# The causal mask of an attention kernel, added by TensorE into the scores' bank instead of by VectorE in its maximum

## The reference: three mixers in one layer, two of them attention

```python
def safe_softmax(s, mask):
    s = jnp.where(mask, s.astype(jnp.float32), NEG_INF)
    m = jnp.max(s, axis=-1, keepdims=True)
    e = jnp.where(mask, jnp.exp(s - m), 0.0)
    return e / jnp.maximum(jnp.sum(e, axis=-1, keepdims=True), 1e-30)
...
    s = (jnp.einsum('bqhd,bshd->bhqs', qb, k).astype(jnp.float32) * ATTN_SCALE
         + cb[..., None] - c[:, :, None, :])
    mask = s_pos[None, :] <= t[:, None]
    p = safe_softmax(s, mask)
    return jnp.einsum('bhqs,bshd->bqhd', p, v).astype(q.dtype)
```

## Time and profile before

| | |
|---|---|
| time, median of 3 runs | 481.15 us (481.06 to 481.26) |
| the profiled execution's own time | 481.06 us |
| its span | 479.3 us (1.8 us lie outside it) |
| busy | TensorE 448.9 us (94%), weight loads 337.2, VectorE 309.1 (64%), ScalarE 249.8, GpSimd 75.1 |
| mean granted TensorE clock | 0.972 of full |
| nsa's attention | about 162 to 237 us |
| fox's attention | about 336 to 377 us |

### The profile page before, as it was taken

One profiled execution on the slowest core, in us unless ns is written; L12 is line 12 of the kernel. 1 busy time (PEld: TensorE's weight loads), 2 busy tenths in 40 slices (PEclk: granted clock), 3 DMA queues, 4 the chain that ended last, 5 costly groups with the idle time before them and its releaser, 6 DMA issues.

```text
span 479.3 us, 6533 instructions
## 1 busy us (share of the span) xinstructions
PE 448.9 (94%) x2232; PEld 337.2 (70%) x2232; DVE 309.1 (64%) x655; ACT 249.8 (52%) x472; POOL 75.1 (16%) x122
## 2 busy tenths in 40 slices
PE   5899999999869889999999999999799996999997
PEld 1576778788758665656577897988666675788885
DVE  5976469887987977777428854758867367522204
ACT  5555685667464666666528865842566435312200
POOL 4011240000000155556300000000354200000000
PEclk9899999999979989999999999999799998899999
DMA  7722234331141200000011242642200011922004
GB/s 260 290 89 88 88 89 131 102 118 45 44 133 44 88 2 1 1 3 0 2 44 45 88 125 96 166 144 83 93 2 1 1 43 55 335 94 88 0 1 175
DMA packets 12960, 39.52 MB, mean 82 GB/s; under 512 B 1792, under 2 KB 2048, under 8 KB 12672
## 3 DMA queue, kind: packets, MB, share of 16 engines
q1 hardware_dynamic: 12928, 39.11, 25.1%
HBM read 32.81 MB, written 2.10 MB: 73 GB/s over the span
## 4 chain that ended last, share of the span: by engine, by line
PE 75%; DVE 14%; issue 4%; ACT 3%; POOL 1%; DMA 1%; SPq 1%; POOLq 0%; DVEq 0%; ACTq 0%
PE bank L1112 10%; PE bank L1114 10%; PE bank L1113 10%; PE bank L1225 6%; PE bank L1207 5%; PE bank L1325 5%; PE bank L1326 4%; PE bank L1327 4%; PE bank L1198 4%; PE bank L1199 3%; DVE wl L767 2%; PE bank L1123 2%; PE bank L1092 2%; PE bank L1142 2%; PE bank L1094 2%
## 5 line engine op out<-in xcount | busy, mean ns | idle before, releaser
L1112 PE MATMUL bank<-xh,wh 128*128 128x512 f32 (+1 forms) x264 | 111.9, 424 | 0.0
L1114 PE MATMUL bank<-xh,wl 128*128 128x512 f32 (+1 forms) x264 | 104.1, 394 | 0.0
L1113 PE MATMUL bank<-xl,wh 128*128 128x512 f32 (+1 forms) x264 | 103.6, 392 | 0.0
L767 DVE TENSOR_TENSOR wl<-raw,wh 128x1024 fp32r<-128x1024 f32 x51 | 62.0, 1219 | 34.5 <-ACT wh L502 34.1
L502 ACT ACTIVATE wh<-raw 128x1024 fp32r<-128x1024 f32 x51 | 53.1, 1049 | 35.3 <-PE bank L1327 35.1
L952 DVE CUSTOM_DVE_ANT_0 bank<-bank,mask_row 128x128 f32<-128x128 f32 (+3 forms) x96 | 47.1, 495 | 24.1 <-PE bank L1199 23.5
L1112 PEld LDWEIGHTS bank<-xh,wh 128*128 128x128 f32 (+1 forms) x264 | 49.7, 188 | 15.0 <-issue 5.0
L1113 PEld LDWEIGHTS bank<-xl,wh 128*128 128x128 f32 (+1 forms) x264 | 49.4, 187 | 14.4 <-issue 4.0
L1114 PEld LDWEIGHTS bank<-xh,wl 128*128 128x128 f32 (+1 forms) x264 | 49.3, 187 | 11.7
L470 POOL TENSOR_SCALAR probs<-probs,rcp,gates 128x128 f32<-128x128 f32 (+3 forms) x52 | 31.7, 617 | 125.8 <-DVE rcp L968 125.6
L610 ACT ACTIVATE probs<-bank,negmax 128x256 f32<-128x256 f32 (+3 forms) x77 | 40.5, 527 | 20.0 <-DVE negmax L952 19.2
(11 more groups left out here) (199 smaller groups left out, 766.5 us busy)
## 6 DMA issues: line engine op xcount, KB each, us to landing
raw<-in_w_in SPq DMA_DIRECT2D x39, 512.0 KB, 3.4
raw<-in_w_out SPq DMA_DIRECT2D x12, 512.0 KB, 3.3
x_raw<-in_xT SPq DMA_DIRECT2D x8, 256.0 KB, 6.2
x_res<-in_x_tok SPq DMA_DIRECT2D x1, 2048.0 KB, 8.2
out_y<-y_out SPq DMA_DIRECT2D x8, 256.0 KB, 2.1
cmp_w_sb<-in_cmp_w SPq DMA_DIRECT2D x1, 1024.0 KB, 10.3
kh_fox<-kh_fox SPq DMA_DIRECT2D x8, 128.0 KB, 2.3
kl_fox<-kl_fox SPq DMA_DIRECT2D x8, 128.0 KB, 2.4
```

Source lines behind the costliest of these rows:

```text
L767: dve.tensor_tensor(wl[:, c % HL, :], raw[:, c % RAW, :], wh[:, c % HL, :].bitcast(F32), ALU.subtract).then_inc(wl_ready, 1)
L1112: pe.matmul(dst, hi, xh[:, k, :], start=(k == 0), stop=False)
L1113: pe.matmul(dst, hi, xl[:, k, :], start=False, stop=False)
L1114: mm = pe.matmul(dst, lo, xh[:, k, :], start=False, stop=(k == KT - 1))
```

## The change

The mask moves from VectorE's fused operation to a third (for fox a fourth) matmul in the same accumulation, and VectorE's operation becomes a plain maximum.

- TensorE: after L1199 a matmul of the identity (`ident_r`) with the causal triangle (`mask_r`), both 128 x 128 in fp32r, is added to the last 128 of the unit's n columns; `s_ready` is now given by it. 96 more matmuls with their weight loads.
- VectorE: a TENSOR_REDUCE (maximum, negated) that reads the bank and writes one number a row takes the place of the fused operation and its accumulator read: 96 instructions for 192. The bank is not written.
- ScalarE: the exponential loses its scale of -1.
- Set-up: `mask_row` is gone; `ones` has 128 columns of its own, GpSimd clears 384 columns less, VectorE makes `ident_r` and `mask_r` right after the second chunk's split, and the copy of the triangle at L1003 is gone.

```diff
-        mask_row = sb("mask_row", [P, SEQ])
-        ones = mask_row[:, SEQ - P:]
+        ones = sb("ones", [P, P])
+        ident_r = sb("ident_r", [P, P], F32R)
+        mask_r = sb("mask_r", [P, P], F32R)
...
-            nc.gpsimd.memset(mask_row[:, 0:SEQ - P], 0.0)
...
-                act.activation(probs_of(u, 0, n), SCORE[u % S_RING][:, 0:n], ACT.Exp, scale=-1.0,
+                act.activation(probs_of(u, 0, n), SCORE[u % S_RING][:, 0:n], ACT.Exp,
...
-                        scores = SCORE[s % S_RING][:, 0:n]
-                        dve.tensor_tensor_reduce(scores, scores, mask_row[:, SEQ - n:], scale=-1.0, scalar=3.0e38,
-                                                 op0=ALU.add, op1=ALU.min,
-                                                 accum_out=negmax[:, s % M_RING:s % M_RING + 1])\
-                           .then_inc(max_ready, 1)
+                        dve.tensor_reduce(negmax[:, s % M_RING:s % M_RING + 1], SCORE[s % S_RING][:, 0:n], AX.X,
+                                          ALU.max, negate=True).then_inc(max_ready, 1)
...
             dve.wait_ge(const_loaded, 16)
+            dve.tensor_copy(ident_r[:, :], ident)
+            dve.tensor_copy(mask_r[:, :], cst[:, CAUSAL:CAUSAL + P])
...
-            dve.tensor_copy(mask_row[:, SEQ - P:], cst[:, CAUSAL:CAUSAL + P])
...
-                pe.matmul(dst[:, 0:n], q, kl[:, 0:n], start=False, stop=True).then_inc(s_ready, 1)
+                pe.matmul(dst[:, 0:n], q, kl[:, 0:n], start=False, stop=False)
+                pe.matmul(dst[:, t * P:n], ident_r[:, :], mask_r[:, :], start=False, stop=True).then_inc(s_ready, 1)
```

More of the change, by code:

```diff
@@ L448, in _ @@
         def _(pool):
-            nc.gpsimd.memset(ones, 1.0).then_inc(ones_ready, 1)
+            nc.gpsimd.memset(ones[:, :], 1.0).then_inc(ones_ready, 1)
             nc.gpsimd.memset(eps1[:, :], EPS)
@@ L1253, in _ @@
                     square = qr[:, i % 2, :]
-                pe.matmul(MEAN[:, :], ones, square, start=(k == 0),
+                pe.matmul(MEAN[:, :], ones[:, :], square, start=(k == 0),
                           stop=(k == KT - 1)).then_inc(x_sq_used, 1)
```

## The result

The changed kernel takes 482.23 us (480.94 to 483.91), the kernel before, on the same chip, 479.55 us (478.02 to 481.29). The ratio is 1.0053, with a 95% interval of 1.0039 to 1.0068: 2.6 us slower, where 5.9 were forecast. The sign was right and the size was more than twice too large. Of the 4.8 us between the forecast's 487.0 and 482.23, 1.6 lie in its base: 481.15 was the median of three runs of the kernel before, and twenty give 479.55.

What follows compares the result with a forecast made beforehand. TensorE was taken to bound the settled pairs, VectorE having some 2 us slack. Masks 8.58, waits -1.7, VectorE -0.4 gave 6.5, shaded to 5.9; 481.1 + 5.9 = 487.0 us, range 483.0 to 490.5.

Steps and rivals of the forecast that it cites:

- One mask matmul: TensorE, each unit's added mask: 0.11 us at full clock whatever n is, 0.22 at half clock; 8.58 us for 71.
- lower bound: Mask matmul on TensorE: 0.06 us if only 128 columns stream and the weight load hides behind the matmul ahead.
- Nothing moves: Rival: a mask costs 0.06 us on TensorE and all waits return, giving about 482 us; chance 0.06.
- signs of being wrong: Pairs keeping their length, mask piece of 0.06 or 0.22, a stage's beginning without a 0.50-clock stretch, or a new one.
- back-to-back issue gap: Skill figure for TensorE: some 81 ns per sustained 128-column load and matmul; would make 71 masks about 2.4 us less.
- what TensorE gets back: Settled nsa pairs: transposes' waits for GpSimd shrink by 0.31 us a pair over 5.5 pairs, -1.7 us.
- fox's own 0.16: Fox pairs' transpose waits, 0.16 us over 2.1 pairs, counted only in the bound of -2.9 us.
- The shade of 0.6: Sum lowered by 0.6 us, from 6.5 to 5.9, towards the full return of TensorE's waits.
- VectorE, -0.4: Stage beginnings and ends: 0.05 us less latency for each of about eight maxima on the chain, -0.4 us.
- the clock stays up: Rival: masks keep TensorE at 2.4 GHz at stage beginnings, nsa 1.6 us, fox 3.1; middle 484 us, chance 0.11.
- the set-up: Before attention: VectorE's first work shifts by up to 0.4 us, covered by 1.4 us of projections; cost 0.

Runs made afterwards that it cites:

- the pads: Changed kernel with an unused tile of 4 or 64 bytes a partition ahead of the identity, moving later tiles: 484.34 us (1.0098) and 484.08 us (1.0089).
- VectorE's half alone: Changed kernel without the mask matmul: plain maximum, causal mask inside the diagonal block left out; 479.82 us, 0.9997 of the kernel before.
- the first masks-only kernel: Changed kernel with VectorE's old fused operation on a 4-byte zero column, which moved large tiles by 32 bytes; 485.46 us (1.0104), again 485.33 us (1.0114).
- the masks-only kernel in its right place: Mask matmuls with VectorE's old operation, zero column cut from a 512-byte tile so large tiles keep their place; 482.01 us, 1.0041 of the kernel before.
- the second comparison: The changed kernel run once more against the kernel before, nothing else changed, with another profile; 481.72 us, 1.0043.
- the kernel meant to beat both: Mask matmul (bfloat16) and plain maximum only in units where TensorE's chain is passed by, old operation with mask row elsewhere; 479.99 us, 1.0001 of before.

## Why the prediction was wrong in size

**Failed: "One mask matmul", 0.11 whatever n is.** This is the term that was mis-sized. The nearest row, the second scores matmul of a 128-key unit, was the right one for a mask behind 128 columns, and only there. Its 0.11 is what a matmul costs when the one ahead streams too short a time to cover its load, so it already depended on the neighbour and not on the matmul itself. I had written the other case down as the lower bound: 0.06 if "the weight load hides behind the matmul ahead". Since six of eight units stream 256 to 512 columns ahead of the mask, that bound was the rule. At half clock a mask was 0.11 and not 0.22, for the same reason; the chain at fox's beginning, with a scores matmul of 512 keys ahead of it:

```profile
343.72 0.43 PE bank L1197
344.15 0.11 PE bank L1198
```

The chain of after holds 73 masks, 5.45 us of them, against 8.58 for 71: 3.1 us too much, nearly the whole miss in the difference. By the ratio the forecast's 481.15 became 483.7, 3.3 below 487.0; the rest of the miss is the base. The rival that comes nearest is "Nothing moves", which had 0.06: it priced the mask at 0.06 and ended at about 482. Its +1.4 is too low, since masks behind 128 columns cost 0.11 and not all the waits went. Two of the prediction's own signs of being wrong were there to be seen, the mask piece of 0.06 and a stage's beginning without a stretch at 0.50.

The sentence on the skill went wrong beside it. By the Trainium skill ("TensorE: Matmul & The Clock Gate", section LDWEIGHTS) I let the load set this matmul. The trace agrees behind 128 columns (0.11) and with the doubled mask (0.11), and differs behind 256 and more (0.06), where the load is hidden. The agreement is one with the spacing in the chain only: the records of these loads themselves last 195 ns in the mean, not an estimated 107. The figure of its section on the back-to-back issue gap, 81 ns, lies between 0.06 and 0.11, and the 2.4 us that it took off the sum would have been nearer than my 0.11. Worked out again they are about 2.3 (64 x 0.029, and 7 x 0.058 at half clock).

**Held: what TensorE gets back.** 0.31 a pair was forecast for nsa, and some 0.32 came back, by the mechanism given: three of the four groups now come later than GpSimd's blocks. Of fox's own 0.16, 0.10 came back; I had kept that in the bound only. The shade of 0.6 towards it was about right.

**Not decided: VectorE, -0.4.** With the accumulator reads gone the pairs are no faster, and the time (0.9997, with 0.9982 to 1.0011) can't tell -0.4 from nothing. The chain of nsa's attention suggests 0.1 to 0.3: 82.71 us for 82.84 without masks, and with them 83.40 to 83.52 in four profiles (the changed kernel's two and those with the pads) against 83.62 to 83.75 in the three with the old operation. From a bank the plain maximum takes 280 ns for 128 columns and 422 for 256, close to the fused form's 434:

```profile
L951 DVE TENSOR_REDUCE negmax<-bank 128x1 f32<-128x256 f32 x24 | 10.1, 422 | 8.4 <-PE bank L1198 8.4
L951 DVE TENSOR_REDUCE negmax<-bank 128x1 f32<-128x128 f32 x24 | 6.6, 280 | 2.2 <-PE bank L1198 2.1
```

**Open, as a rival: the clock stays up.** I gave it 0.11 for both stages together and put 1.6 us on nsa's beginning. It came in nsa, in each profile with masks. From the last projection to the first whole values group of nsa the chain took 13.95 us before and 12.92 after: 1.0 us. In fox 340 to 344 us stand at 0.50 in both, but that can't be put down to the change. VectorE's half alone, which has no masks either, spent 3.4 us there at half clock where before spent 6.8; the first masks-only kernel had none in one profile and 3.4 us (342.5 to 345.9) in the other; and the masks-only kernel in its right place had none, so that the same 4 us read:

```profile
340.00:344.00 4.00, 3.48 (x22) 2.77 (x22) 3.95 (x14) 1.89 (x7) 2.64 (x4) 1.00 0.23 91
```

Nor do the times show a whole stretch won. If 3.4 us at half clock were gone from every execution of the changed kernel, its mean granted clock would be higher by some 1.7 / 480 = 0.0035; over all executions it is 0.9817 (35) against 0.9807 (56). So the 1.0 us is the difference of these profiles, and the kernel as a whole has perhaps a third of it.

**Held: the set-up.** The projections keep their pace, and the stretch between the two attentions is 79.70 us before and 79.71 after.

**The sum again, with what was measured:** 5.45 of masks, -1.7 for nsa's waits, -0.3 for fox's, 0 for VectorE, -1.0 for nsa's beginning: +2.5 us. The ratio gives +2.6. That they agree so well is luck. In the second comparison the ratio was 1.0043, +2.1. The chains of the two profiles give +0.6 us for nsa's attention, +1.3 for fox's, -0.6 for the last stage and -0.5 ahead of the attentions, +0.8 in all: 0.6 less in the two attentions than this sum has, and elsewhere the low clock in the profile of before. What is sure is the settled pairs, +0.28 and +0.47 each; the -1.0 is not.

**Open: the last stage.** Behind fox's attention TensorE waits near 404 us and then runs at half clock for a while. These are 402 to 414 us before, then after:

```profile
402.00:414.00 12.00, 7.66 (x24) 6.00 (x24) 9.23 (x13) 5.86 (x9) 0.00 (x0) 0.72 0.59 223
```

```profile
402.00:414.00 12.00, 7.66 (x27) 5.85 (x27) 9.74 (x14) 5.87 (x9) 0.00 (x0) 0.86 0.58 228
```

TensorE is busy for the same 7.66 us, but 0.72 means some 6.8 us at half clock and 0.86 some 3.4. In the thirteen profiles the stretch has one of these two lengths, and the first masks-only kernel shows the short one in its first profile and the long one in its second, so it can differ between executions of one program. With the short one (five, both of the changed kernel among them) the chain from fox's end to the end of the kernel is 90.5 to 91.0 us, with the long one (eight, that of before among them) 91.3 to 92.1. It isn't simply the masks, since six profiles of kernels that have some show the long one, that of the kernel meant to beat both too; there it cost most of what the attention had won. The 0.6 and 0.8 us by which the changed kernel's last stage is shorter in its two profiles are thus seen and not explained, and with them the medians could not be told to better than that.

## What to carry to other kernels

In these traces a small matmul put onto a full TensorE cost its own stream (0.06 us for 128 columns), or what its weight load stuck out behind the stream ahead of it (0.11), whichever was longer. Price it from a row with the same neighbour, not from one with the same shape, and put it behind the widest matmul there is: the same three matmuls in another order cost 2.4 us more. Look at the granted clock of the execution that was profiled before two traces are subtracted from each other. Look for waits that an added instruction can slip into, since they pay it back. And when an experiment needs a new tile, however small, declare it so that the large tiles keep their addresses, or its place will be measured as its effect.

## What the runs showed of the hardware

Moving the large tiles of one kernel by 32 or 64 bytes made matmuls of 512 columns follow each other every 0.233 or 0.232 us instead of 0.229, and the kernel some 2.5 us longer than its own 481.7 to 482.2, with no instruction changed. I hadn't expected an address to show in TensorE's pace.

A bfloat16 weight load of 128 columns took 98 ns in the mean and one in rounded fp32 195; in the chain that was 0.07 against 0.11 or 0.12 us behind 128 columns, and no gain behind wider ones (0.07 and 0.06).

With masks at nsa's beginning, beside other engines' work, TensorE stayed at its full 2.4 GHz from 162 to 182 us in eleven profiles of eleven; without them it had 3.4 us at 1.2 GHz there in two of two. At fox's beginning and in the last stage the same program showed such stretches of different length in two executions.

The mean granted clock of one kernel's executions went from 0.972 to 0.986, and its time from about 481.2 us to about 478.5 with it.
